# Adding the second scale's modulation by whole rows, and clearing three accumulators on GpSimd

## The reference, cut to what matters

```python
def first_block(x, c, ada_w, ada_b, ...):
    c_act = jax.nn.silu(c)
    mod = c_act @ ada_w[l] + ada_b[l]
    sh1, sc1, g1, sh2, sc2, g2 = jnp.split(mod, N_MOD, axis=-1)
    h = rms_norm(x, mix_pre_g[l]) * (1.0 + sc1[:, None, :]) + sh1[:, None, :]
    y = hybrid_mixer(h, w_in[l], ..., w_out[l])          # attention and convolution, then w_out
    x = x + g1[:, None, :] * rms_norm(y, mix_post_g[l])
    h = rms_norm(x, ffn_pre_g[l]) * (1.0 + sc2[:, None, :]) + sh2[:, None, :]
    y = swiglu_ffn(h, w_gate[l], w_up[l], w_down[l])
    x = x + g2[:, None, :] * rms_norm(y, ffn_post_g[l])
```

## Time and profile before

| | us |
|---|---|
| median of 3 runs | 2593.62 |
| lowest and highest run | 2590.73 and 2597.53 |
| profiled execution, its own time | 2600.93 |
| profiled execution, its span | 2598.9 |
| TensorE busy in the span | 2544.0 (98%) |
| VectorE busy | 1824.3 (70%) |
| ScalarE busy | 1300.3 (50%) |
| GpSimd busy | 152.6 (6%) |

### The profile page before, as it was taken

One profiled execution on the slowest core, in us unless ns is written; L12 is line 12 of the kernel. 1 busy time (PEld: TensorE's weight loads), 2 busy tenths in 40 slices (PEclk: granted clock), 3 DMA queues, 4 the chain that ended last, 5 costly groups with the idle time before them and its releaser, 6 DMA issues.

```text
span 2598.9 us, 37676 instructions
## 1 busy us (share of the span) xinstructions
PE 2544.0 (98%) x13172; PEld 2096.5 (81%) x13172; DVE 1824.3 (70%) x2264; ACT 1300.3 (50%) x1860; POOL 152.6 (6%) x260
## 2 busy tenths in 40 slices
PE   7999999899999999999999999999999999999999
PEld 4787887778888888887888888887888888888887
DVE  2348869778898887988755565555588866667565
ACT  2349755534444444465624242425465555655553
POOL 3111111011200000000001010100000000000000
PEclk9999999999999999999999999999999999999999
DMA  9989878689888888788464545454488856656654
GB/s 354 387 312 369 232 280 304 200 307 354 280 293 268 269 268 281 269 307 289 139 205 155 185 151 189 151 189 139 151 268 288 271 176 190 189 170 209 193 193 166
DMA packets 236751, 622.96 MB, mean 240 GB/s; under 512 B 20284, under 2 KB 24679, under 8 KB 231776
## 3 DMA queue, kind: packets, MB, share of 16 engines
q1 hardware_dynamic: 213392, 525.40, 61.1%
q0 software_dynamic: 22448, 91.84, 10.3%
q10 hardware_dynamic: 800, 4.25, 0.4%
HBM read 613.80 MB, written 7.60 MB: 239 GB/s over the span
## 4 chain that ended last, share of the span: by engine, by line
PE 82%; DMA 8%; DVE 6%; ACT 2%; issue 2%; SPq 0%; DVEq 0%; POOL 0%; ACTq 0%
PE ps L2339 12%; PE ps L2279 12%; PE ps L2281 11%; PE ps L2280 11%; PE ps L2341 6%; PE ps L2744 6%; PE ps L2746 6%; PE ps L2745 5%; DMA slot<-in_ada_w 3%; PE ps L2314 2%; DMA raw<-in_w_down 2%; PE ps L2318 2%; PE ps L2316 2%; DVE w_lo L1412 2%; PE ps L2665 1%
## 5 line engine op out<-in xcount | busy, mean ns | idle before, releaser
L1412 DVE TENSOR_TENSOR w_lo<-raw,w_hi 128x1024 fp32r<-128x1024 f32 x762 | 929.0, 1225 | 545.3 <-ACT w_hi L764 543.8
L764 ACT ACTIVATE w_hi<-raw 128x1024 fp32r<-128x1024 f32 x762 | 804.9, 1058 | 958.7 <-PE ps L2281 378.4
L2339 PE MATMUL ps<-h_both,w_hi 128*128 128x512 f32 (+1 forms) x1392 | 483.0, 393 | 1.4 <-DVE x L1764 0.7
L2279 PE MATMUL ps<-w_hi,h_both 128*128 128x512 f32 x1152 | 463.0, 402 | 6.1 <-DVE h_both L1501 3.7
L2281 PE MATMUL ps<-w_hi,h_both 128*128 128x512 f32 x1152 | 449.5, 390 | 0.0
L2280 PE MATMUL ps<-w_lo,h_both 128*128 128x512 f32 x1152 | 449.0, 390 | 0.0
L2341 PE MATMUL ps<-h_both,w_lo 128*128 128x256 f32 (+1 forms) x1392 | 386.7, 278 | 0.0
L2339 PEld LDWEIGHTS ps<-h_both,w_hi 128*128 128x128 f32 x1392 | 262.3, 188 | 59.7 <-DVE h_both L1501 0.9
L1424 DVE SCALAR_TENSOR_TENSOR acc<-ada,cact,acc 128x1024 f32<-128x1024 f32 x224 | 288.6, 1288 | 7.8 <-DMA ada<-in_w_ada 2.7
L2744 PE MATMUL ps<-w_hi,f_hi 128*128 128x512 f32 x680 | 265.5, 390 | 2.0 <-DVE z_up L2155 1.1
L2745 PE MATMUL ps<-w_lo,f_hi 128*128 128x512 f32 x680 | 264.6, 389 | 0.0
(11 more groups left out here) (284 smaller groups left out, 3090.3 us busy)
## 6 DMA issues: line engine op xcount, KB each, us to landing
ada<-in_w_ada SPq DMA_DIRECT2D x192, 512.0 KB, 4.3
raw<-in_ffn_w_up SPq DMA_DIRECT2D x160, 512.0 KB, 4.5
slot<-in_ada_w POOLq DMA_DIRECT2D x60, 1024.0 KB, 9.3
raw<-in_na_w_qkv SPq DMA_DIRECT2D x96, 512.0 KB, 4.7
raw<-in_w_gate SPq DMA_DIRECT2D x88, 512.0 KB, 5.1
raw<-in_w_up SPq DMA_DIRECT2D x88, 512.0 KB, 4.9
raw<-in_w_down SPq DMA_DIRECT2D x88, 512.0 KB, 5.5
raw<-in_ffn_w_down SPq DMA_DIRECT2D x86, 512.0 KB, 4.6
```

What stands on the lines that cost most here:

```text
L764: act.activation(w_hi[:, s, :], raw[:, s, :], ACT.Copy).then_inc(hi_ready, 1)
L1412: dve.tensor_tensor(w_lo[:, s, :], raw[:, s, :], w_hi[:, s, :].bitcast(F32), ALU.subtract).then_inc(lo_ready, 1)
L2279: pe.matmul(o, hi_[:, k, a], wh, start=(k == 0), stop=False)
L2339: pe.matmul(ps[:, 4 * part + g, :].rearrange("p (a n) -> p a n", a=2)[:, :, n], w_hi[:, s, a], h_both[:, :, k, n], start=(k == 0 and ts[-1 ...
```

## The change

1. **Units become rows.** `scale_unit` becomes `scale_row`: one operation over all 2048 columns of row k. 32 operations become 16. The step tables put three rows beside the last value tiles (steps 2, 4, 6), four beside attention (u = 0, 2, 4, 6) and nine beside the rest of the out projection (m = 11, 13, 15, 17, 19, 22, 24, 26, 28).
2. **Loads of 1 MB.** GpSimd issues 16 loads of 1 MB instead of 32 of 512 KB; the load of row k waits until row k-2 is done.
3. **Clears.** The three clears ahead of FFN tiles 9 and 10 go from VectorE to GpSimd, which does them as soon as `x_ready` is 2, ahead of the bias rows that need them.

```diff
-        SC2_LN, SC2_ATT, SC2_OUT = 5, range(PER_GROUP), range(11, KD + 14)
+        SC2_LN, SC2_ATT, SC2_OUT = (2, 4, 6), (0, 2, 4, 6), (11, 13, 15, 17, 19, 22, 24, 26, 28)
...
-            for u in range(UNITS):
-                src = ins["ada_w"][0][u // 2 * P:(u // 2 + 1) * P, 4 * D + u % 2 * TILE:4 * D + (u % 2 + 1) * TILE]
-                if u < 4:
-                    pool.wait_ge(group_done, GROUPS - 2 + u // 2)
+            for k in range(KD):
+                src = ins["ada_w"][0][k * P:(k + 1) * P, 4 * D:5 * D].rearrange("p (c n) -> p c n", c=2)
+                if k < 2:
+                    pool.wait_ge(group_done, GROUPS - 2 + k)
                 else:
-                    pool.wait_ge(ada_used, UNITS * 4 + u - 1)
-                pool.dma_start(scale_w[u // 2 % 2][:, u % 2, :], src).then_inc(scale_landed[u % 4], 16)
+                    pool.wait_ge(ada_used, UNITS * 4 + 2 * k)
+                pool.dma_start(scale_w[k % 2][:, :, :], src).then_inc(scale_landed[k % 2], 16)
...
+            pool.wait_ge(x_ready, NT)
+            for acc in (acc0, acc1, tmp):
+                pool.memset(acc[:, :], 0.0).then_inc(acc_clear, 1)
             bias_row(2, 0, "ada_b", 5)
...
-            pool.wait_ge(x_ready, NT)
...
-            def scale_unit(u):
+            def scale_row(k):
...
+                dve.scalar_tensor_tensor(out=acc_s[:, :], in0=scale_w[k % 2][:, :, :].rearrange("p c n -> p (c n)"),
+                                         scalar=cact[:, k:k + 1], in1=acc_s[:, :],
+                                         op0=ALU.mult, op1=ALU.add).then_inc(ada_used, 2)
...
-                clear(acc0)
                 for j in range(9, CT + 3):
-                    clear((acc1, tmp)[j - 9])
                     lo(Tend, j)
```

More of the change, by code:

```diff
@@ L203, in program @@
         group_done = sem("group_done")
-        scale_landed = [sem(f"scale_landed{i}") for i in range(4)]
+        scale_landed = [sem(f"scale_landed{i}") for i in range(2)]
         scale_bias = sem("scale_bias")
@@ L326, in o_first @@
             return (o_a_hi[:, m, :], o_a_lo[:, m, :]) if m < 2 else (o_hi[:, m, :], o_lo[:, m, :])
-        SC2_LN, SC2_ATT, SC2_OUT = 5, range(PER_GROUP), range(11, KD + 14)
-        assert SC2_LN + len(SC2_ATT) + len(SC2_OUT) == UNITS
+        SC2_LN, SC2_ATT, SC2_OUT = (2, 4, 6), (0, 2, 4, 6), (11, 13, 15, 17, 19, 22, 24, 26, 28)
+        assert len(SC2_LN) + len(SC2_ATT) + len(SC2_OUT) == KD
         def conv_rounds(step):
@@ L1430, in unit @@
                 ins_.then_inc(ada_used, 1)
-            def scale_unit(u):
[L1434 to L1438, removed]
+            def scale_row(k):
+                dve.wait_ge(scale_landed[k % 2], 16 * (k // 2 + 1))
+                dve.wait_ge(ada_used, UNITS * 4 + 2 * k + 2)
+                dve.scalar_tensor_tensor(out=acc_s[:, :], in0=scale_w[k % 2][:, :, :].rearrange("p c n -> p (c n)"),
+                                         scalar=cact[:, k:k + 1], in1=acc_s[:, :],
+                                         op0=ALU.mult, op1=ALU.add).then_inc(ada_used, 2)
             def clear(acc):
@@ L1702, in second_scale @@
                     dve.wait_ge(scale_bias, 16)
-                if n in (2, 3, 4, 6, 7):
-                    scale_unit((2, 3, 4, 6, 7).index(n))
+                if n in SC2_LN:
+                    scale_row(SC2_LN.index(n))
             for i in range(2):
@@ L1895, in beside_out1 @@
                 if u in SC2_ATT:
-                    scale_unit(SC2_LN + SC2_ATT.index(u))
+                    scale_row(len(SC2_LN) + SC2_ATT.index(u))
             def later_sc2(m):
                 if m in SC2_OUT:
-                    scale_unit(SC2_LN + len(SC2_ATT) + m - SC2_OUT[0])
+                    scale_row(len(SC2_LN) + len(SC2_ATT) + SC2_OUT.index(m))
             softmax(PER_GROUP, M["att1"], NT, causal, None, beside_out1, tight=True)
```

## The result

| | before | after |
|---|---|---|
| median of 20 runs each, side by side, us | 2596.44 | 2602.0 |
| lowest and highest run | 2590.26 and 2601.69 | 2597.15 and 2610.16 |
| ratio of the medians, with its 95% interval | | 1.0021 [1.0013, 1.0029] |
| profiled execution, its own time and its span | 2600.93 and 2598.9 | 2597.15 and 2595.4 |

After is 5.6 us slower (3.4 to 7.5 by the interval), inside the 0.3% that counted as no change. The forecast was a loss of 2.7 us, inside 0.3%. The two profiled executions say the opposite: after's is the shorter by 3.8 us. So the spans can't be compared, and I compare pieces of the trace.

The account below looks back on a forecast made before the run. TensorE was taken to bound the kernel, VectorE a few per cent behind in attention and out projection. 0 + 3.9 - 0.6 + 1.0 - 1.6 = +2.7 us on 2593.62 gave 2596.3 us, range 2587.5 to 2603.5.

Parts of the forecast that it names:

- Part 1: VectorE's row operation over 2048 columns: 2.34 us, bounds 2.28 and 2.56, against 1.28 for a unit.
- Part 2: Beside the last value tiles: three rows replace five units, 0.6 us more for VectorE, costed at nothing.
- Part 3: Beside attention: rows delay the scaling in even steps, odd steps give nothing back; +3.9 us, between -0.2 and +4.7.
- Part 4: Rest of the out projection: wait behind tile 21 goes, late rows offset other gains; -0.6 us, between -2.3 and +1.8.
- Part 5: Boundary: GpSimd's first memset holds VectorE's CAST and TensorE with it; +1.0 us, between 0 and +4.7.
- Part 6: Clears' old place ahead of FFN tiles 9 and 10: first gate unit and loads 1.6 us sooner; -1.6, between -2.3 and 0.
- the forecast's own bound: Whole kernel: the forecast's terms at their limits, from 2592.7 to 2601.1 us; forecast's chance 0.52.
- the stalled boundary: Rival at the boundary: three memsets without a gap hold the CAST 4.7 us, clock adds 2; 2602.0 us, chance 0.10.
- the late rows: Rival in the out projection: late rows cost the full 5.6 us and delay tile loads; 2601.9 us, chance 0.10.
- attention absorbs the rows: Rival in attention: hidden slack takes up the rows, -0.2 us instead of +3.9; 2592.2 us, chance 0.20.
- everything is given back: Rival: all waits for `w_lo` and the probabilities go, 6.3 us, with the CAST unheld; 2587.3 us, chance 0.08.

Follow-up runs that it names:

- clears_only: Before, with only the three clears moved to GpSimd as in after; 2594.61 us against 2596.14, ratio 0.9998.
- units_late: Before, units kept, with the three clears on GpSimd behind the last split of the new `h`; 2597.2 us against 2596.16, ratio 1.0008.
- rows_only: After, with the three clears back on VectorE at their old place; 2598.53 us against before's 2596.14, ratio 1.0017.
- late_clears: After, with GpSimd's three clears moved behind the last split of the new `h`; 2598.63 us against before's 2596.16, ratio 1.0011.
- odd_steps: After, with the four attention rows in steps 1, 3, 5, 7 instead of 0, 2, 4, 6; 2599.6 us against before's 2596.14, ratio 1.0008.
- no_rows_att: After with clears behind the last split, the four attention row additions left out, loads kept; 2597.06 us against before's 2597.81, ratio 0.9992.
- the second comparison: An unchanged copy of after, run again beside before; 2602.62 us against 2597.81, ratio 1.0011.
- loads_only: Before, units kept, with sixteen 1 MB loads that each wait for both units of row k-2; 2601.86 us against 2596.14, ratio 1.0021.
- halves_late: After with clears behind the last split, each attention row cut into two halves, one per step; 2595.76 us against before's 2596.16, ratio 0.9999.
- places: Before with late GpSimd clears, units moved off attention step 0 and tile 21; 2595.62 us against 2597.81, ratio 0.9994; repeat 2593.68 against 2595.66, 0.9989.

## Why the prediction was right, point by point

**Part 1 held.** A row takes 2.35 us, where 1.28 + 1.06 = 2.34 was worked out.

**Part 2 held.** No wait of TensorE lies between 340 and 380 us in after either.

**Part 3 held in its mechanism, and its size was right but for one term.** TensorE's timeline in after, the transposes of the even steps and of one odd step (404.75), idle time before them in brackets:

```profile
391.01 0.69 PE L2691 MATMUL ps<-ident,prob 128*128 128x128 f32 x2 [2.54 <-DVE prob L1644]
...
400.84 0.44 PE L2691 MATMUL ps<-ident,prob 128*128 128x128 f32 x2 [0.87 <-DVE prob L1644]
...
404.75 0.38 PE L2691 MATMUL ps<-ident,prob 128*128 128x128 f32 x2
...
409.64 0.44 PE L2691 MATMUL ps<-ident,prob 128*128 128x128 f32 x2 [0.87 <-DVE prob L1644]
...
418.43 0.44 PE L2691 MATMUL ps<-ident,prob 128*128 128x128 f32 x2 [0.87 <-DVE prob L1644]
```

That is 1.5 + 1.06 at u = 0, and three times 0.87 where about 1.0 was predicted. The idle time understates the cost: from one step's transposes to the next's, an even step takes 4.89 us (409.64 - 404.75) in place of 3.87 to 3.91 before, 1.0 more, as predicted. And VectorE shows that the odd steps give nothing back. One even step (u = 2), the odd step behind it (from 400.70) and the maximum that opens the next even one:

```profile
396.16 0.42 DVE L1631 CUSTOM_DVE_ANT_0 prob<-ps,causal 128x256 f32<-128x256 f32 x1 [2.92 <-PE ps L2654]
...
397.98 2.35 DVE L1438 SCALAR_TENSOR_TENSOR acc_s<-scale_w,cact,acc_s 128x2048 f32<-128x2048 f32 x1
...
400.43 0.35 DVE L1644 TENSOR_SCALAR prob<-prob,stat 128x256 f32<-128x256 f32 x1
400.70 0.42 DVE L1631 CUSTOM_DVE_ANT_0 prob<-ps,causal 128x256 f32<-128x256 f32 x1
...
402.71 0.35 DVE L1644 TENSOR_SCALAR prob<-prob,stat 128x256 f32<-128x256 f32 x1
404.95 0.42 DVE L1631 CUSTOM_DVE_ANT_0 prob<-ps,causal 128x256 f32<-128x256 f32 x1 [1.89 <-PE ps L2654]
```

The maximum at 396.16 has waited 2.92 us for the scores (with the half clock below), and that of the next even step 1.89, where before the maxima of steps 2 to 7 each waited 0.25 to 0.35. The odd step's own maximum starts at once; what VectorE saves in that step it spends idle ahead of the next. Two steps take 8.80 us (409.64 - 400.84) in place of 7.7. The whole stage went from 43.56 to 47.39 in the second profile: +3.83, where +3.9 was predicted. By the starts of the transposes that is 1.07 up to the first, 2.99 in the three even steps, 0.11 in the odd ones and 0.34 back in the last; the waits alone, which grew by 3.4, don't show it all. In the first profile the stage took 48.85, and the further 1.46 is **the term I missed**: behind the 2.54 us wait TensorE's granted clock falls to 0.50 of full speed, the 1.2 GHz level. After, in pieces of 2 us (clock, DMA share and GB/s are the last three numbers):

```profile
388.00:390.00 2.00, 0.47 (x3) 0.07 (x1) 2.00 (x2) 0.20 (x1) 0.00 (x0) 1.00 0.46 141
390.00:392.00 2.00, 0.99 (x4) 0.89 (x5) 1.97 (x6) 0.26 (x1) 0.53 (x1) 0.70 0.31 121
392.00:394.00 2.00, 2.00 (x6) 1.58 (x5) 1.20 (x4) 1.86 (x5) 0.00 (x0) 0.50 0.95 266
394.00:396.00 2.00, 2.00 (x10) 1.58 (x9) 0.00 (x0) 0.00 (x0) 0.00 (x0) 0.95 0.94 354
```

That is (0.30 + 0.50 + 0.05) x 2 = 1.7 us lost. The prediction looked at the clock only at the boundary, and didn't ask what a wait grown from 1.5 to 2.5 us would do.

**Part 4 held in sum, and its fear was half right.** The wait of 0.60 us behind tile 21 is gone. The stage went from 63.82 and 63.21 to 62.47 and 63.32, -0.6 in the mean, as predicted, though the single values lie 0.9 us apart. The other kernels agree: `clears_only` and `units_late`, by units, take 63.95 and 63.45; `rows_only`, `late_clears`, `odd_steps` and `no_rows_att`, by rows here, 62.33 to 63.76. VectorE's late rows are there: 4.8 us idle in 4 pieces ahead of them, which the profile puts down to "issue", for instance

```profile
462.85 2.35 DVE L1438 SCALAR_TENSOR_TENSOR acc_s<-scale_w,cact,acc_s 128x2048 f32<-128x2048 f32 x1 [0.96 <-issue]
469.43 2.35 DVE L1438 SCALAR_TENSOR_TENSOR acc_s<-ada,cact,acc_s 128x2048 f32<-128x2048 f32 x1 [1.96 <-issue]
```

It is most likely the landing: the row at 469.43 was asked for at 459.92, and in `late_clears` a wait of 1.34 us at the place of another of the four is put down to the load. 5.6 us were feared for VectorE. TensorE feels only the last: its `w_lo` wait of 1.5 us ends at 473.07, behind the row that starts at 469.43.

**Part 5 held.** GpSimd's memsets of 128 x 2048 in after's timeline:

```profile
491.16 3.69 POOL L702 MEMSET acc<- 128x2048 f32 x2 [29.60 <-DVE x L1800]
494.79 2.15 POOL L702 MEMSET tmp<- 128x2048 f32 x1
```

The first two take about 1.85 us each (1.8 was estimated; 1.82 is the mean in `late_clears`, where VectorE doesn't disturb them). The first starts at 491.16 and so ends at about 493.0; the CAST starts at 492.15, behind a `lo` that ran beside the memset at its usual 1.22 us, and ends at 493.11. It is held for 0.68 us and TensorE with it, where 1.0 was predicted: it came 0.99 us behind the memset's start where I had placed it 0.8 behind. By the Trainium skill, "SBUF — State Buffer", section "Who interferes with whom", the CAST is held by a GpSimd instruction, and an operation with two SBUF inputs is not held by one that reads no SBUF. The trace agrees: the CAST took 0.96 us in place of 0.28, and its remainder, with two inputs and beside the second memset, 0.43 in place of 0.42. The rival that three memsets run in a row before VectorE gets in fell: it got in behind the first, and again for `diag`.

**Part 6 came out in the trace, but is not shown to be the clears' doing.** The second gate's first unit starts 31.5 us behind the boundary's first FFN matmul in place of 33.3 (1.6 sooner was predicted), and the waits for `w_lo` fell from 2.3 to 0.2. But a second profile of before had 1.4, and `rows_only`, with the clears on VectorE, had none and a stage of 160.36 us. Once the clock's losses are taken off, this stage took between 159.1 and 163.5 us in fourteen executions. The four with the clears on VectorE reach from 160.4 to 163.5 (mean 161.6), the four with them on GpSimd at `x_ready` from 159.1 to 160.2 (mean 159.8), and the six with them later on GpSimd from 160.1 to 163.4 (mean 161.5). The first unit does start sooner without the clears on VectorE: 29.1 to 30.7 us behind the first FFN matmul in ten executions against 31.1 to 31.8 in four, with the clock's losses off. So an earlier unit is shown, and a gain for TensorE of the predicted size is possible with the early clears, but the scatter within a kind is as large, and the timed runs of `clears_only` (0.9998, give or take 0.1%) are too coarse to tell. Why the stage varies I don't know. The prediction read one execution's waits as something the change could win; it should have asked for a second one.

**The sum.** By the marks, after is slower by 1.8 us in the mean of two profiles each (281.97 against 280.17), where 2.7 was forecast: +4.6 in attention (3.8 for the rows, the rest the clock of one profile), -0.6 in the out projection, +0.7 at the boundary and -2.8 in the FFN stage (rounded). The timed loss is 5.6 us (3.4 to 7.5) in the first comparison and by the ratio 2.9 (-0.5 to 6.0) in the second. The forecast of 2.7 lies below the first interval and inside the second: direction and smallness were right, the size was too low by up to 3 us. Two terms are in doubt: the clock behind the first wait, which was put at nothing and cost 1.5 us in one profile of two, and part 6's gain of 1.6, which the timed runs don't show. If that gain is scatter, the marks without the FFN stage give +4.6 us, which agrees with the timed loss, but that reading is argued and not shown. The rest I could not locate: outside the marks the same matmuls run, and single executions scatter there by about as much. The mean clock of every run doesn't settle it. Taken as (1 - clock) x time, after's runs in the second comparison lost 11.9 us to it and before's beside them 10.7, but `rows_only`, with the same rows, lost only 9.5 against 10.7.

The absolute time was less well met. It was reckoned from 2593.62 us, the median of three runs; over twenty, before's median is 2596.44, 2.8 us more, and the larger loss adds as much again. So after came out at 2602.0 and not 2596.3, above the forecast's own bound of 2601.1 and just where two rivals had put it, the stalled boundary (2602.0) and the late rows (2601.9). Neither happened. That the forecast and not one of them is borne out rests on the traces; the time alone would have named the wrong one.

**The rivals.** That attention absorbs the rows fell (5.1 us of waits, and 5.6 us back when the rows are left out). That everything is given back fell for this change, though other places for the units do it. That the clears stall the boundary fell in size (0.7 us), and late rows in effect on TensorE. `loads_only` shows that the last was near: with the units kept, the late loads cost 0.21%.

## What to carry to other kernels

Where two engines run a step in lockstep, merging two operations into one of twice the length costs in the step it lands in, most where the other engine already waits, and the step it leaves gives almost nothing back: 3.8 us lost here with less work done. Merge loads only together with what uses them: a 1 MB load that waited for two users cost as much here as the whole change. Before counting on a wait's disappearance, look at the same wait in a second execution. And where several theories give nearly the same time, let their traces decide.

## What the hardware showed that I had not expected

The same idle time of TensorE, 2.54 to 2.57 us at the first attention step, brought the half clock in two executions (after, `rows_only`: 1.7 us lost each) and not in two others (after's second profile and `late_clears`), where the clock stayed at 1.00. TensorE's timeline of the second profile of after, with a wait as long as the first one's:

```profile
390.77 0.44 PE L2691 MATMUL ps<-ident,prob 128*128 128x128 f32 x2 [2.54 <-DVE prob L1644]
```

and its clock there:

```profile
390.00:392.00 2.00, 1.23 (x7) 1.05 (x8) 1.97 (x6) 0.75 (x3) 0.53 (x1) 1.00 0.56 141
392.00:394.00 2.00, 2.00 (x10) 1.67 (x9) 0.95 (x4) 1.37 (x4) 0.00 (x0) 1.00 0.80 279
```

The wait for `diag` at the boundary says the same more broadly: it is 2.25 or 2.26 us long in all fourteen executions, and the clock fell to 0.50 behind it in six (`rows_only`, `clears_only`, `loads_only`, `units_late`, `halves_late` and the repeat of `places`) and stayed up in eight. So the length of the wait alone doesn't decide it, and what does, these runs don't show. Between the first mark and the last, executions lost 1.7, 3.4 or, once, 5.1 us to the clock; the 5.1 was in `clears_only`, whose span was nonetheless among the shortest.

The other engine is held too where GpSimd and VectorE exclude each other: the third memset took 2.15 us in place of 1.82 (in `late_clears`), beside VectorE's second CAST, which took 0.85 in place of 0.43.
